# A hybrid decoder step: the value convolution of the first four feed-forward pairs in two PSUM banks, and ScalarE's order around the last pair

## The reference, cut to what matters

```python
def conv_ffn(xn, buf, w_up, cw, cb, w_down):
    up = xn @ w_up                                  # 1024 -> 2 * 2816
    upc, new_buf = causal_dwconv(up, buf, cw, cb)   # width 3, by channel
    val, gate = jnp.split(upc, 2, axis=-1)
    return (jax.nn.gelu(gate) * val) @ w_down, new_buf
```

## Time and profile before

| | us |
|---|---|
| median of three runs | 1045.46 (1044.52 to 1046.51) |
| the profiled execution | 1043.88 |
| its span, first to last instruction | 1042.1 |
| PE busy in the span | 1013.1 |
| first product with w_up begins | 620.1 |
| first down product, D(0,0), begins | 691.0 |
| D(4,1), the first product behind the last pair, begins | 987.9 |
| end of the last down product | 1028.3 |

### The profile page before, as it was taken

How to read it: one execution, slowest core, us unless ns; L and a number is a source line. 1 busy time by engine, 2 the same in 40 slices (tenths; PEclk the granted TensorE clock), 3 DMA queues, 4 the chain that set the end, 5 groups by cost and what they waited for, 6 DMA issues and landing times.

```text
span 1042.1 us, 20026 instructions
## 1 busy us (share of the span) xinstructions
PE 1013.1 (97%) x7688; PEld 988.9 (95%) x7688; DVE 743.4 (71%) x1270; ACT 520.4 (50%) x936; POOL 420.6 (40%) x286
## 2 busy tenths in 40 slices
PE   8999999999999999999999989899999999999985
PEld 7899999999999999999999988899999999999985
DVE  6788457956746567385635799998888787878654
ACT  7576787314343444442522456655555545555553
POOL 4333334333222223233133446666454545454430
PEclk9999999999999999999999998999999999999997
DMA  8633432478487686783652422323232323232137
GB/s 199 191 85 94 106 79 76 104 190 220 91 241 200 141 257 146 191 228 93 207 187 80 125 61 82 102 62 112 72 112 71 113 71 112 72 107 76 36 93 217
DMA packets 263268, 132.95 MB, mean 128 GB/s; under 512 B 82720, under 2 KB 257045, under 8 KB 262920
## 3 DMA queue, kind: packets, MB, share of 16 engines
q1 hardware_dynamic: 262966, 131.63, 46.1%
q10 hardware_dynamic: 210, 0.07, 0.0%
HBM read 104.17 MB, written 25.29 MB: 124 GB/s over the span
## 4 chain that ended last, share of the span: by engine, by line
PE 80%; DVE 8%; issue 5%; DMA 2%; POOL 2%; ACT 1%; SPq 0%; DVEq 0%; POOLq 0%; ACTq 0%
PE ring L2747 40%; PE bank L3138 11%; PE ring L3152 10%; PE ring L3138 9%; PE bank L2989 2%; PE bank L2793 1%; POOL wlo L1226 1%; DVE bank L1880 1%; DMA d_stage<-in_w_down 1%; POOL f_lo L1269 1%; PE bank L2972 1%; PE bank L3069 1%; PE bank L2900 1%; PE bank L3057 1%; DMA y<-out_rows 1%
## 5 line engine op out<-in xcount | busy, mean ns | idle before, releaser
L1226 POOL TENSOR_TENSOR wlo<-stage,whi 128x1024 fp32r<-128x1024 f32 x78 | 197.6, 2534 | 397.3 <-ACT whi L1282 397.3
L2747 PE MATMUL ring<-x_split,whi 128*128 128x322 f32 (+2 forms) x1952 | 347.5, 300 | 0.0
L2747 PEld LDWEIGHTS ring<-x_split,whi 128*128 128x128 f32 x1952 | 294.5, 189 | 8.9 <-issue 8.1
L2747 PE MATMUL ring<-x_split,wlo 128*128 128x256 f32 (+1 forms) x976 | 210.4, 297 | 0.0
L2747 PEld LDWEIGHTS ring<-x_split,wlo 128*128 128x128 f32 x976 | 164.6, 189 | 0.0
L1282 ACT ACTIVATE whi<-stage 128x1024 fp32r<-128x1024 f32 x79 | 83.4, 1055 | 93.7 <-PE ring L2747 77.5
L1269 POOL TENSOR_TENSOR f_lo<-f_stage,f_hi 128x512 fp32r<-128x512 f32 x78 | 103.9, 1348 | 57.5 <-ACT f_hi L1663 57.5
L1269 POOL TENSOR_TENSOR f_lo<-d_stage,f_hi 128x512 fp32r<-128x512 f32 (+1 forms) x48 | 57.8, 1204 | 119.2 <-ACT f_hi L1663 119.1
L3138 PE MATMUL bank<-fx_T,f_hi 128*128 128x290 f32 x264 | 79.3, 301 | 4.4 <-DVE ring L2609 4.2
L1663 ACT ACTIVATE f_hi<-f_stage 128x512 fp32r<-128x512 f32 x112 | 69.0, 628 | 27.8 <-PE bank L3138 25.9
L3138 PE MATMUL bank<-fx_T,f_lo 128*128 128x290 f32 x264 | 78.3, 297 | 0.0
(11 more groups left out here) (430 smaller groups left out, 2359.1 us busy)
## 6 DMA issues: line engine op xcount, KB each, us to landing
stage<-in_w_in SPq DMA_DIRECT2D x56, 512.0 KB, 4.2
f_stage<-in_w_up SPq DMA_DIRECT2D x44, 512.0 KB, 5.3
d_stage<-in_w_down SPq DMA_DIRECT2D x40, 256.0 KB, 2.8
stage<-in_w_branch_a SPq DMA_DIRECT2D x8, 512.0 KB, 3.6
c_sample<-in_state_mlstm_C SPq DMA_DIRECT2D x16, 256.0 KB, 6.5
out_s_mlstm_C<-c_sample SPq DMA_DIRECT2D x16, 256.0 KB, 2.4
stage<-in_w_branch_b SPq DMA_DIRECT2D x8, 512.0 KB, 3.8
stage<-in_w_out SPq DMA_DIRECT2D x8, 512.0 KB, 3.8
```

What stands on the lines that cost most here:

```text
L1226: pool.tensor_tensor(spaced(wlo[:, slot]), packed(stage[:, slot, 0:n]), spaced(whi[:, slot]).bitcast(F32), ALU.subtract).then_inc(w_lo, 1)
L2747: last = pe.matmul(of(z, t0 or -2, t1), w[:, kk * WS:kk * WS + P], x_, start=kk == 0 and m == 0, stop=kk == kn - 1 and m == 2)
```

## The change

Four things are done. For pairs 0 to 3 (`i < LAG - 1`, LAG is 5) the value's taps are made in `wide[1]` in place of `val_taps`, and gelu writes `val_taps` in place of the gate's own place; later pairs are as before. PE gets one more wait, ahead of D(0,0): for the product of pair 3. In the pass of the last pair the two history copies and the gate's first tap move ahead of the rounding of D(5,1)'s piece. After the loop gelu and the value's first tap come ahead of the roundings for D(4,3) and D(5,3), and `product_hi` comes ahead of those for D(4,4) and D(5,4).

```diff
--- before.py
+++ after.py
@@ -707,6 +707,15 @@
 
         pool_ = bank[:, :, :].rearrange("p h t -> p (h t)")
         cv = (val_taps[:, 0:CV_N], pool_[:, 0:CV_N])
+
+        def value_conv(i):
+
+            return wide[1][:, 0:CV_N] if i < LAG - 1 else cv[0]
+
+        def gelu_out(i):
+
+            return cv[0] if i < LAG - 1 else cv[1]
+
         sample_product = pool_[:, CV_N:CV_N + TD - SEQ]
         acc_a = (bank[:, 2, 0:QT], bank[:, 3, 0:QT])
         acc_b, acc_c = ring[:, 0, 0, 0:QT], ring[:, 0, 1, 0:QT]
@@ -1757,14 +1766,14 @@
                 act.wait_ge(hist_done, 2 * i + 2)
                 if i:
                     act.wait_ge(g_lo if j else prod_done, i)
-                act.activation(cv[j], up[:, j, 0:CV_N], ACT.Identity,
+                act.activation(cv[1] if j else value_conv(i), up[:, j, 0:CV_N], ACT.Identity,
                                scale=cols[:, C_FCW[0] + ft:C_FCW[0] + ft + 1], bias=cols[:, C_FCB + ft:C_FCB + ft + 1]
                                ).then_inc(tap_done, 1)
 
             def gelu(i):
 
                 act.wait_ge(gate_conv, i + 1)
-                act.activation(cv[1], cv[1], ACT.Gelu_apprx_tanh).then_inc(gelu_done, 1)
+                act.activation(gelu_out(i), cv[1], ACT.Gelu_apprx_tanh).then_inc(gelu_done, 1)
 
             def product_hi(i):
 
@@ -1801,11 +1810,15 @@
                 ahead("T2", i)
                 if 0 < i < NPAIR - 1:
                     product_hi(i - 1)
+                if i == NPAIR - 1:
+                    history(i, 0)
+                    history(i, 1)
+                    first_tap(i, 1)
                 ahead("B22", i)
                 if d:
                     ahead("D", d[0], d[1] + 1)
                 ahead("T3", i)
-                if i:
+                if 0 < i < NPAIR - 1:
                     history(i, 0)
                     history(i, 1)
 
@@ -1821,14 +1834,13 @@
                                scale=cols[:, C_FG + m:C_FG + m + 1]).then_inc(fin_gain, 1)
 
             i, g0, g1 = NPAIR - 1, GROUPS - 2, GROUPS - 1
-            first_tap(i, 1)
+            gelu(i)
+            first_tap(i, 0)
             ahead("D", g0, 0)
-            gelu(i)
             ahead("T4", i)
-            first_tap(i, 0)
+            product_hi(i)
             ahead("D", g0, 1)
             ahead("D", g0, 2)
-            product_hi(i)
             ahead("D", g1, 0)
             ahead("D", g1, 1)
             square(0)
@@ -2617,7 +2629,7 @@
 
             def other_taps(i, j):
 
-                ft, U, c_ = i + UPT // 2 * j, up[:, j], cv[j]
+                ft, U, c_ = i + UPT // 2 * j, up[:, j], cv[1] if j else value_conv(i)
                 w = [cols[:, C_FCW[m] + ft:C_FCW[m] + ft + 1] for m in range(FW)]
                 dve.wait_ge(tap_done, TAPPED["gate" if j else "value", i])
                 st.link(mul_add(c_, U[:, 1:1 + CV_N], w[1], c_))
@@ -2631,9 +2643,9 @@
 
                 dve.wait_ge(gelu_done, i + 1)
                 dve.wait_ge(val_conv, i + 1)
-                st(tt(grouped(sample_product, LS), sample_conv(val_taps[:, :]), sample_conv(cv[1]), ALU.mult))
+                st(tt(grouped(sample_product, LS), sample_conv(value_conv(i)), sample_conv(gelu_out(i)), ALU.mult))
                 st.wait()
-                tt(cv[1][:, 0:SEQ], cv[0][:, 0:SEQ], cv[1][:, 0:SEQ], ALU.mult).then_inc(prod_done, 1)
+                tt(cv[1][:, 0:SEQ], value_conv(i)[:, 0:SEQ], gelu_out(i)[:, 0:SEQ], ALU.mult).then_inc(prod_done, 1)
 
             def product_lo(i):
 
@@ -3162,6 +3174,7 @@
                 if d:
                     if d == (0, 0):
                         pe.wait_ge(act_once, ACT_ONCE["frms"])
+                        pe.wait_ge(prod_done, LAG - 1)
                     else:
                         pe.wait_ge(tile_evicted, down_out_count(8 * d[0] + d[1]))
                     down_product(*d)
```

## The result

The changed kernel took 1048.85 us (median of 7 runs, 1048.17 to 1050.97); the kernel before, run beside it, 1046.42 (7 runs). The ratio is 1.0032 with a 95% interval of 1.0021 to 1.0044, or +3.3 us (2.2 to 4.6): slower by 0.3%. The forecast was +0.5.

What follows compares the result with a forecast made beforehand. PE, busy 97% of the span, was taken as the bound, so only its waits could be won. Terms -0.9 - 3.3 + 3.3 + 0.1 + 1.3 = +0.5 us gave a median of 1046.0 us, range 1043.0 to 1048.0.

Steps and rivals of the forecast that it cites:

- Value taps: Early rounds: value taps in PSUM no longer stretch beside POOL, shortening PE's waits for VectorE; -0.9 us, bounds 0 and 1.5 won.
- the lower bound's reason: Early rounds: nothing is won if the wait for POOL moves to another SBUF operation of VectorE, such as a weight sum.
- The wait ahead of D(0,0): PE's new wait for pair 3's product, with 0.28 us to spare: costs 0 to 0.3 us, taken as 0.
- PE 3.3 us earlier at the transposes, and not through: Tail: waits for C21 (0.8) and gl (2.5) go, but PE waits the 3.3 us off at the transposes.
- The slip: Tail: D(5,1)'s later rounding delays loads up to D(4,5), making D(4,6)'s load, square and down_evict late by +0.1 us.
- the upper bound: Tail: +1.1 us if the full delay from D(5,1)'s later rounding stays in the chain of loads.
- The clock: Behind PE's new idle of about 3.8 us at the transposes the clock falls: +1.3 us, bounds 0 and 2.7.
- The sum: Whole kernel: -0.9 - 3.3 + 3.3 + 0.1 + 1.3 = +0.5 us.
- the tail's chain grows longer: Rival, tail: full slip +1.1 and full clock loss 2.7, sum +2.9, 1048.4 us; decided above 3.0 us lost; chance 0.10.
- The base: Median of the runs of the kernel before, 1045.46 us, from which the forecast for the median was made.
- the clock holds: Rival, tail: all as forecast without the clock's +1.3, since two idles of 2.5 us cost nothing; 1044.7 us; chance 0.30.

Runs made afterwards that it cites:

- e9: Changed kernel with the last pair's gate tap behind D(5,1)'s rounding and value tap behind D(4,3)'s; ratio to the kernel before 0.9989.
- e10: Changed kernel with 36 further identity transposes on PE filling its wait ahead of the seven transposes; ratio to the kernel before 0.9989.
- e13: Second look at the changed kernel with only the last pair's gate tap behind D(5,1)'s rounding; ratio to the kernel before 0.9997.
- e3: Changed kernel with ScalarE's square(0) and square(1) ahead of the roundings of D(4,5), D(5,5) and D(4,6); ratio to the kernel before 0.9970.
- e4: Changed kernel with the seven transposes moved behind D(4,4) and D(5,4) on PE; ratio to the kernel before 0.9968.
- e7: Changed kernel with VectorE's down_evict(5, m + 1) ahead of its transpose of feature m; ratio to the kernel before 0.9978.
- e5: The changed kernel run again without any edit; ratio to the kernel before 1.0008.
- e12: Second look at e9, both taps of the last pair behind the roundings in the changed kernel; ratio to the kernel before 0.9989.
- e2: Kernel before with only the change's ScalarE loop and tail order, value taps still in SBUF; ratio to the kernel before 1.0039.
- e8: e7 with ScalarE's squares as early as possible, turned-row copies ahead of the last two roundings, two feature stores between the last loads; 1040.69 us against 1047.03.
- e1: Changed kernel with ScalarE's loop and tail as before, so only the early value taps in PSUM; ratio to the kernel before 0.9987.
- e14: The kernel before run again without any edit; one launch, 48.14 us from the copy of T2(21) to the end of the last down product.

## Why the prediction was wrong

**Value taps, -0.9: right.** -1.1 us from the first C22 to the copy in ten of the thirteen traces with the taps in PSUM (338.78 to 338.88, against 339.96 and 339.95 in the two traces of before). In the other three (e9, e10, e13) only 0.3 to 0.5 us was won; in e10 a weight sum took 1.79 us and PE waited 1.57. That is the lower bound's reason, seen in some launches. PE's waits for L2621 are 3.3 us in sum, as the prediction said.

**The wait ahead of D(0,0), 0: right.** No row of the view of waits names it.

**PE 3.3 us earlier at the transposes, and not through: right.** It came 23.86 us after the copy (1011.69 - 5.37 - 982.46) against 27.70, 3.8 us earlier, and then waited for ScalarE's squares behind the roundings, as forecast; e3, e4 and e7 show each link.

**The slip, +0.1: wrong, and this is the step that failed.** It measured +1.1 in after and +0.9 in e5, at the upper bound. The path was right: after's chain goes from the late D(5,1) through the loads, roundings and rests of D(4,3), D(4,4) and D(4,5). These are their loads (chain that ended last, after: start, duration, what):

```profile
990.45 2.77 DMA d_stage<-in_w_down
...
995.49 2.87 DMA d_stage<-in_w_down
...
1000.41 2.95 DMA d_stage<-in_w_down
```

The size was wrong. The prediction let a delay of 1.05 us (997.5 against 996.45) run through this chain unchanged and had 0.8 of it covered: before, D(4,5)'s load landed at about 999.15 and its rounding was held until 999.95 by PE's late D(5,0). That left 0.25 by its own numbers (1000.2 - 999.95), of which it took 0.1. The cover held, but the delay grew on its way. D(5,1) was rounded 1.1 us late as forecast, D(4,4) 1.6 and not 1.0 to 1.2 (15.92 after the copy, against 14.31), and D(4,5) at 1003.38, which in before's time (2.36 earlier) is 1001.0. Two things that the prediction had put at nothing made it grow. The three loads, priced at one row of 2.7 us, took 2.77, 2.87 and 2.95 us, where before they took 2.7, 2.6 and 2.7. And POOL's rest of D(4,3) took 1.51 us in place of 1.29 (POOL before; then POOL and VectorE after):

```profile
990.43 1.29 POOL L1269 TENSOR_TENSOR f_lo<-d_stage,f_hi 128x512 fp32r<-128x512 f32 x1 [1.08 <-ACT f_hi L1663]
```

```profile
993.95 1.51 POOL L1278 TENSOR_TENSOR f_lo<-d_stage,f_hi 128x512 fp32r<-128x512 f32 x1 [2.42 <-ACT f_hi L1672]
992.59 1.70 DVE L1892 SCALAR_TENSOR_TENSOR val_taps<-up,cols,val_taps 128x592 f32<-128x592 f32 x2 [0.95 <-ACT val_taps L1769]
```

The change had moved the last pair's value taps, with two SBUF inputs, beside that rest; with the value's tap behind D(4,3)'s rounding the rest takes 1.30 and 1.31 us again (e9, e12). It is the conflict that the prediction saw in the early pairs and left out here. Why the loads took 0.1 to 0.3 us longer in after is not shown.

**The clock, +1.3: right in kind, low.** 1.5 and 2.1 us in the two traces of after, 2.7 in e2; e10 shows that it is PE's idle time. The half of 2.7 that the prediction took is the low end of what came. Its remark that PEclk is 1.00 behind the wait of 2.5 us is right, but the earlier trace rows do not hold that stretch; this is it (before, columns as there):

```profile
1000.00:1005.00 5.00, 5.00 (x40) 5.00 (x40) 2.36 (x9) 2.64 (x5) 2.03 (x2) 1.00 0.27 79
```

The Trainium skill, page "TensorE: Matmul & The Clock Gate", section "HAM oscillation — how this bites in real kernels", has idle time in one piece paid for by a cold start; the traces agree for all seven waits of 3.8 to 5.4 us.

**The sum.** With the measured terms it is -1.1 + 1.0 (mean of 1.1 and 0.9) + 1.8 (mean of 1.5 and 2.1) = +1.7 us in place of +0.5. Of the two comparisons one lies above (+3.3, 2.2 to 4.6), and the other has it inside its interval (+0.8, -0.4 to 2.1). The launches' starts, which move the first C22 by up to 5.5 us in any version, are of the size of this difference, but that they made it is not shown. The nearest of the cases is the rival "the tail's chain grows longer": the slip came in full, the clock at 1.5 and 2.1 and not at its 2.7, so tail and clock together lost 2.6 and 3.0 us where the rival asked for over 3.0. It had 0.10, because I leaned on a cover of 0.8 us against a delay that I took as fixed.

**The base.** 1045.46 was the median of three runs; before measured 1046.42, 1047.03, 1047.35 and 1047.62 beside later runs. On the highest of these the forecast +0.5 alone would have left the range, which ended at 1048.0. The later runs were made on several chips, and no run tells chip from launch.

## What to carry to other kernels

Time won ahead of a wait is kept only if what releases the next wait moves as well: walk that chain back through every engine's program order, and look for a quick instruction (a square, an evict) that stands behind one waiting for a load. Put the quick releasing instruction first, or the waiting one later: here two single moves of the first kind (e3, e7) took the time to 3.1 and 2.3 us under before, one of the second kind (e4) to 3.4, and the first two with two smaller ones (e8) to 6.6. And where a delay enters a chain of loads, ask at each link what now runs beside it, and price the loads by their slowest rows, before counting on a cover of less than 1 us.

## What the runs showed of the hardware

- **The order of two starts decides who waits.** VectorE's squaring, with two SBUF inputs, took 1.23 us when it began 0.16 us ahead of POOL's rest, and 3.33 when it began 0.11 behind it; POOL's rest then took 3.31 or 2.37. The other 14 traces are alike: 1.22 or 1.23 where VectorE began first or at the same time, 3.25 to 3.43 where POOL did. The Trainium skill, page "SBUF — State Buffer", section "Who interferes with whom", says that such a pair excludes each other by order of issue; the rows agree.
- **Short idle times can cost clock too, but not always.** Behind 2.14 us (e1, waiting for `gl`) PEclk was 0.70 in the window from 1000 to 1005, and behind 2.45 us (e2) 0.66 from 670 to 675; behind 2.45 and 2.54 (before), 2.58 (e14) and 2.04 us (e3) it stayed at 1.00. The prediction's "the clock holds", built on two idles of 2.5 us, rested on luck.
- **A 256 KB load took 2.6 to 4.5 us** at one place of the tail, longest (4.2 and 4.5) in the two traces where a 0.02 MB packet of the instruction queue started 1 us after it; the cause is not shown.
